# A ring of expert weights with nine places instead of eight, its first places refilled by quarters, and fewer filler products around the last chunk of a mixing

## The reference

```
# first block
merged = sigmoid(mg_h) * (o_h @ w_br_hg) + sigmoid(mg_n) * (o_n @ w_br_nsa)
y = (1 + g1) * (merged @ w_out)
x = layer_norm(ALPHA * x + y) * ln1_g + ln1_b
h = layer_norm(x) * (1 + sc2) + sh2
y = (1 + g2) * hier_moe(h)              # 32 experts, hidden width 512
x = layer_norm(ALPHA * x + y) * ln2_g + ln2_b
# second block
x = x + gt_m * (concat(attn_out, pool_out) @ w_out)
h = modulate(rmsnorm(x, norm_ffn_g), sh_f, sc_f)
x = x + gt_f * hierarchical_moe(h)      # 32 experts, hidden width 256
return rmsnorm(x, norm_final_g)
# both mixtures
group   = argmax of 4 group logits; 2 best of its 8 experts; weight = p_group * softmax(2 logits)
expert  = (silu(h @ w1[e]) * (h @ w3[e])) @ w2[e]
```

## Time and profile before

| what | value |
|---|---|
| median of 3 runs (lowest, highest) | 1993.25 us (1984.94, 2000.85) |
| the profiled execution, and its span | 1992.76 us, 1990.9 us |
| mean granted TensorE clock in it | 0.945 of full speed |
| busy: TensorE products, VectorE, ScalarE, GpSimd | 1742.8, 763.2, 431.6, 103.2 us |
| bytes moved by the DMA engines, mean rate | 474.79 MB, 238 GB/s |
| issued by SP's queue | 398.66 MB |
| one slice of expert weights | 2048 KB, 27.8 to 33.8 us from issue to landing |
| first mixing and its experts, products from, to | 844, 1416 us |
| second mixing and its experts, products from, to | 1629, 1967 us |

### The profile page before, as it was taken

One profiled execution on the slowest core, in us unless ns is written; L12 is line 12 of the kernel. 1 busy time (PEld: TensorE's weight loads), 2 busy tenths in 40 slices (PEclk: granted clock), 3 DMA queues, 4 the chain that ended last, 5 costly groups with the idle time before them and its releaser, 6 DMA issues. The chain is left out here.

```text
span 1990.9 us, 22057 instructions
## 1 busy us (share of the span) xinstructions
PE 1742.8 (88%) x8104; PEld 994.4 (50%) x8104; DVE 763.2 (38%) x1907; ACT 431.6 (22%) x1072; POOL 103.2 (5%) x127
## 2 busy tenths in 40 slices
PE   4999997988998999998977887877889899897886
PEld 2655554445666888747323323333358555632332
DVE  5344445473556654454101111011545454221115
ACT  3323222203445000012201101010122340121122
POOL 1100000000000000000000000000000000011110
PEclk8999997989999999998989989999999999898898
DMA  9533234771111622354999999999611223599995
GB/s 374 192 136 117 96 147 175 266 270 62 40 40 52 231 108 85 144 237 164 383 421 426 427 427 427 427 426 425 246 43 69 86 108 160 205 414 424 424 423 213
DMA packets 68055, 474.79 MB, mean 238 GB/s; under 512 B 11359, under 2 KB 12575, under 8 KB 43249
## 3 DMA queue, kind: packets, MB, share of 16 engines
q1 hardware_dynamic: 51200, 398.66, 49.4%
q0 software_dynamic: 15600, 70.61, 9.3%
q10 hardware_dynamic: 1152, 4.19, 0.5%
HBM read 459.53 MB, written 34.11 MB: 248 GB/s over the span
## 5 line engine op out<-in xcount | busy, mean ns | idle before, releaser
L2105 PE MATMUL moe_ps<-moe_up,moe_hg 128*64 128x512 f32 x1536 | 380.9, 654 | 104.4 <-DMA moe_up<-in_exp_gate 42.8
L2105 PEld LDWEIGHTS moe_ps<-moe_up,moe_hg 128*64 128x64 f32 x1536 | 132.8, 150 | 349.0 <-issue 348.7
L490 PE MATMUL hg_proj<-hT,hg_w 128*128 128x512 f32 x384 | 171.6, 605 | 6.1 <-DMA hg_w<-in_w_hg 6.1
L2142 PE MATMUL moe_ps<-moe_down,moe_midT 128*64 128x512 f32 x720 | 162.7, 601 | 15.6 <-DMA moe_down<-in_exp_down 15.0
L2195 ACT ACTIVATE moe_sig<-moe_ps 128x512 f32<-128x512 f32 (+1 forms) x32 | 15.7, 490 | 545.0 <-PE moe_ps L2105 545.0
L2224 DVE COPY moe_midT<-moe_ps 128x512 f32<-128x512 f32 (+1 forms) x32 | 17.8, 557 | 273.1 <-PE moe_ps L2114 273.1
L490 PEld LDWEIGHTS hg_proj<-hT,hg_w 128*128 128x128 f32 x384 | 73.0, 193 | 94.9 <-issue 87.5
L2234 DVE SCALAR_TENSOR_TENSOR moe_res<-moe_ps,moe_route_slot_share,moe_gain 128x512 f32<-128x512 f32 x64 | 45.1, 746 | 162.3 <-PE moe_ps L2142 162.1
L2142 PEld LDWEIGHTS moe_ps<-moe_down,moe_midT 128*64 128x64 f32 x720 | 54.0, 138 | 103.7 <-issue 102.3
L2180 ACT ACTIVATE moe_hg<-moe_ps,mod,scale_ffn 128x128 f32<-128x128 f32 x248 | 89.9, 467 | 49.1 <-PE moe_ps L2088 49.1
L2216 DVE TENSOR_TENSOR moe_mid<-moe_sig,moe_ps 128x512 f32<-128x512 f32 (+1 forms) x32 | 17.7, 555 | 161.0 <-PE moe_ps L2105 158.2
(11 more groups left out here) (409 smaller groups left out, 2520.8 us busy)
## 6 DMA issues: line engine op xcount, KB each, us to landing
moe_down<-in_exp_down SPq DMA_DIRECT2D x45, 2048.0 KB, 29.0
moe_up<-in_exp_up SPq DMA_DIRECT2D x32, 2048.0 KB, 27.8
moe_up<-in_exp_gate SPq DMA_DIRECT2D x32, 2048.0 KB, 29.2
moe_up<-in_exp_in SPq DMA_DIRECT2D x32, 2048.0 KB, 33.8
rest_w<-in_mod_rest POOLq DMA_DIRECT2D x16, 1536.0 KB, 7.3
hg_w<-in_w_hg SPq DMA_DIRECT2D x32, 512.0 KB, 3.6
rest_w<-in_mod_rest POOLq DMA_DIRECT2D x8, 2048.0 KB, 8.5
xn<-in_w_merge SPq DMA_DIRECT2D x32, 512.0 KB, 4.4
```

The lines of the kernel that those rows point to most:

```text
L490: last = pe.matmul(proj[bank][:, :], w[s][:, kc, :], k.hT[:, kc, :], start=(kc == 0), stop=(kc == KC - 1))
L2105: last = pe.matmul(self.up_ps[u][e * SLOTS:(e + 1) * SLOTS, :], self.hg[m % 2][:, kc, e * SLOTS:(e + 1) * SLOTS], w[:, kc, :], start=(kc = ...
L2142: last = pe.matmul(self.res_ps[side][e * SLOTS:(e + 1) * SLOTS, :], self.midT[:, f, e * SLOTS:(e + 1) * SLOTS], w[e][:, f, side * 512:(sid ...
```

## The change

- The ring has nine places (`N_SLOTS`). The mixing's input and weights keep the last three, so six slices are issued when the stage begins, and three after the eighth half.
- Slices 9 and 10, the first that need a place used before, are loaded by `load_pieces` in four quarters each. A quarter is two of the eight blocks of 128 rows of an `up` slice, or one of four of a `down` slice. SP waits for `first_read`, a new semaphore that TensorE raises behind products kc = 1, 3 and 5 of the first pair, and for `up_done0` ahead of the last quarter. TensorE waits for these two slices on semaphores of their own; the counts of places 0 and 1 are one load lower from there on (`times`). SP goes on in the old way from slice 11.
- In the mixing the counts of fillers change: where `affine` is set from 26, 6 and 24 to 12, 3, 5 and 22, the 5 between the turning of the last chunk and its logits. Where it is None they are 8 and 22, and the last chunk is turned ahead of the third chunk's logits.
- The rows of the norms (`load_rows`) are loaded before SP waits for GpSimd's scatters, in place 6 of the ring (first block) or 5 (second); the results go to places 0 and 1, or 3 and 4.
- Room in SBUF: `SMALL` shrinks from 3584 to 2048 bytes of a partition, and the descriptor space of GpSimd's DMAs is set to 4096 bytes of a partition.

The core of the diff:

```diff
...
@@ -1481,8 +1481,8 @@
 KB = 1024
 SLOT = 16 * KB
-N_SLOTS = 8
-SMALL = 7 * 512
+N_SLOTS = 9
+SMALL = 2048
 NOWHERE = 4096
@@ -1649,12 +1649,18 @@
         logits(1)
         turned(2)
         pe.wait_ge(S["part_free"], 2 * TC - 3)
-        self.keep_warm(pe, 26)
-        logits(2)
-        self.keep_warm(pe, 6)
-        turned(3)
+        if self.affine is not None:
+            self.keep_warm(pe, 12)
+            logits(2)
+            self.keep_warm(pe, 3)
+            turned(3)
+            self.keep_warm(pe, 5)
+        else:
+            self.keep_warm(pe, 8)
+            turned(3)
+            logits(2)
         logits(3)
-        self.keep_warm(pe, 24)
+        self.keep_warm(pe, 22)
     def keep_warm(self, pe, n):
@@ -1939,12 +1945,38 @@
         self.last_slot = len(self.slices) - len(downs(PAIRS - 1))
         self.per_slot = [sum(i % N_SLOTS == s for i in range(self.last_slot)) for s in range(N_SLOTS)]
         self.last_w = memory.slot(f"{tag}_last", self.last_slot % N_SLOTS, [P, 2, self.FC, D])
+        self.pieces_loaded = [k.sem(ctx, f"{tag}_pieces_loaded{n}") for n in range(2)]
         self.last_loaded = [k.sem(ctx, f"{tag}_last_loaded{f}") for f in range(self.FC)]
+
+    def piece(self, i, q):
+
+        what, m, u, e = self.slices[i]
+        s = i % N_SLOTS
+        if what == "up":
+            return self.up_w[s][:, 2 * q:2 * q + 2, :], self.up_v[u][2 * m + e][:, 2 * q:2 * q + 2, :]
+        return self.down_w[s][:, q, :], self.down_v[2 * m + q // 2][:, q % 2, :] if e == 2 else self.down_v[2 * m + e][:, q, :]
+
+    def load_pieces(self, sp):
+
+        for q in range(KC // 2):
+            if q < KC // 2 - 1:
+                sp.wait_ge(self.S["first_read"], q + 1)
+            else:
+                sp.wait_ge(self.S["up_done0"], 1)
+            for n, i in enumerate((N_SLOTS, N_SLOTS + 1)):
+                place, source = self.piece(i, q)
+                sp.dma_start(place, source).then_inc(self.pieces_loaded[n], 16)
+
+    def times(self, i, j):
+
+        s = i % N_SLOTS
+        pieced = 1 if s < 2 and (i >= N_SLOTS or not isinstance(j, int)) else 0
+        return j * 16 * self.per_slot[s] + 16 * (i // N_SLOTS + 1 - pieced)
     def load(self, sp, i, j):
         what, m, u, e = self.slices[i]
         if i >= N_SLOTS or not isinstance(j, int):
-            before, n, part, _ = self.slices[i - N_SLOTS]
+            before, n, part, _ = self.slices[i - N_SLOTS if i >= N_SLOTS else self.final_slice(i)]
             done = self.S["down_done" if before == "down" else f"up_done{part}"]
             sp.wait_ge(done, j * PAIRS + (n + 1 if i >= N_SLOTS else n + 1 - PAIRS))
         s = i % N_SLOTS
@@ -1988,9 +2020,13 @@
                 done()
             sums(False)
+    def final_slice(self, s):
+
+        return max(i for i in range(len(self.slices)) if i % N_SLOTS == s)
+
     def emptied(self, sp, s):
-        what, m, u, _ = self.slices[max(i for i in range(len(self.slices)) if i % N_SLOTS == s)]
+        what, m, u, _ = self.slices[self.final_slice(s)]
         sp.wait_ge(self.S["down_done" if what == "down" else f"up_done{u}"], m + 1)
     def sync(self, sp, begin, added):
@@ -2000,6 +2036,8 @@
                 if isinstance(j, int) and i == 2 * N_SLOTS:
                     added.load_tokens(sp)
             if isinstance(j, int):
+                self.emptied(sp, added.rows_place)
+                added.load_rows(sp)
                 sp.wait_ge(self.S["early_stored"], 1)
                 added.load(sp, self.emptied)
@@ -2074,7 +2113,10 @@
         def ready(j, *slices):
             for s in slices:
                 i = self.at[s]
-                pe.wait_ge(self.loaded[i % N_SLOTS], j * 16 * self.per_slot[i % N_SLOTS] + 16 * (i // N_SLOTS + 1))
+                if isinstance(j, int) and N_SLOTS <= i < N_SLOTS + 2:
+                    pe.wait_ge(self.pieces_loaded[i - N_SLOTS], 16 * (KC // 2))
+                else:
+                    pe.wait_ge(self.loaded[i % N_SLOTS], self.times(i, j))
         def turn_rows(j, m):
             pe.wait_ge(self.x_loaded[m % 2], j * 16 * (PAIRS // 2) + 16 * (m // 2 + 1))
@@ -2104,6 +2146,8 @@
                     w = self.up_w[self.at["up", m, u, e] % N_SLOTS]
                     last = pe.matmul(self.up_ps[u][e * SLOTS:(e + 1) * SLOTS, :], self.hg[m % 2][:, kc, e * SLOTS:(e + 1) * SLOTS],
                                      w[:, kc, :], start=(kc == 0), stop=(kc == KC - 1))
+                if isinstance(j, int) and m == 0 and u == 0 and kc % 2 and kc < KC - 1:
+                    last.then_inc(S["first_read"], 1)
             last.then_inc(S[f"up_done{u}"], 1)
         def turn_mid(j, m):
@@ -2287,9 +2331,11 @@
     def __init__(self, k, ctx, tag, memory, banks, experts, residual, affine, scale=None, shift=None, store=None):
         self.k, self.experts, self.residual, self.affine = k, experts, residual, affine
         self.scale, self.shift, self.store, self.ps = scale, shift, store, banks
-        self.y = [memory.at(f"{tag}_y{c}", memory.ring + 8 * c * KB, [P, 2, D]) for c in range(TC)]
-        self.rows = [memory.at(f"{tag}_row{n}", memory.ring + (32 + 4 * n) * KB, [P, D]) for n in range(2 if store is None else 1)]
-        self.junk = memory.at(f"{tag}_junk", memory.ring + 40 * KB, [P, D])
+        self.y_place, self.rows_place = (0, 6) if store is None else (3, 5)
+        y, rows = (memory.ring + place * SLOT for place in (self.y_place, self.rows_place))
+        self.y = [memory.at(f"{tag}_y{c}", y + 8 * c * KB, [P, 2, D]) for c in range(TC)]
+        self.rows = [memory.at(f"{tag}_row{n}", rows + 4 * n * KB, [P, D]) for n in range(2 if store is None else 1)]
+        self.junk = memory.at(f"{tag}_junk", rows + 8 * KB, [P, D])
         n = experts.kept_pairs
         self.onehot = [memory.at(f"{tag}_onehot{m}", k.hT_at + (16 - 2 * (n - m)) * KB, [P, SEQ]) for m in range(n)]
         if store is None:
@@ -2307,19 +2353,17 @@
     def load_tokens(self, sp):
         sp.dma_start(self.onehot[-1][:], self.k.i["tokens"].partition_broadcast(P)).then_inc(self.tokens_loaded, 16)
+    def load_rows(self, sp):
+        for n, row in enumerate(self.rows):
+            sp.dma_start(row[:], self.k.i["norm_rows"][self.affine + n:self.affine + n + 1, :].broadcast_to([P, D])).then_inc(self.rows_loaded, 16)
+
     def load(self, sp, emptied=None):
-        k = self.k
         view = self.experts.results.rearrange("(s c p) d -> c p s d", s=2, p=P)
         for c in range(TC):
             if emptied is not None and c % 2 == 0:
-                emptied(sp, c // 2)
+                emptied(sp, self.y_place + c // 2)
             sp.dma_start(self.y[c][:], view[c]).then_inc(self.loaded[c], 16)
-            if c == 1:
-                if emptied is not None:
-                    emptied(sp, 2)
-                for n, row in enumerate(self.rows):
-                    sp.dma_start(row[:], k.i["norm_rows"][self.affine + n:self.affine + n + 1, :].broadcast_to([P, D])).then_inc(self.rows_loaded, 16)
     def used(self, sp):
@@ -2573,12 +2617,13 @@
             @block.sync
             def _(sp):
                 out.sync(sp)
-                for i in range(5):
+                for i in range(N_SLOTS - 3):
                     experts.load(sp, i, 0)
                 sp.wait_ge(out.S["done"], 2 * TC)
-                for i in range(5, N_SLOTS):
+                for i in range(N_SLOTS - 3, N_SLOTS):
                     experts.load(sp, i, 0)
-                experts.sync(sp, N_SLOTS, added)
+                experts.load_pieces(sp)
+                experts.sync(sp, N_SLOTS + 2, added)
                 added.sync(sp, send_next)
             @block.gpsimd
@@ -3116,7 +3161,7 @@
     from concourse.bass_utils import run_bass_kernel_spmd
     arrays = {f"in_{n}": a for n, a in arrange(**inputs).items()}
-    nc = bacc.Bacc("TRN2", target_bir_lowering=False, num_devices=1)
+    nc = bacc.Bacc("TRN2", target_bir_lowering=False, num_devices=1, dynamic_dma_scratch_size=4096)
     views = {n[3:]: nc.dram_tensor(n, a.shape, mybir.dt.from_np(a.dtype), kind="ExternalInput").ap() for n, a in arrays.items()}
     out = nc.dram_tensor("out_x", (SEQ, D), F32, kind="ExternalOutput").ap()
     program(nc, views, out)
```

2 lines of the change are left out of this document (1 added, 1 removed).

## The result

The changed kernel takes **1970.18 us** in the median of four runs (1965.93 to 1976.26). The kernel before, with one more run in the same comparison, takes 1996.20. The ratio is 0.9889, interval 0.9851 to 0.9928. The prediction was 1970. By the one 22 us are saved, by the other 18. That is clear of noise, and under 2%. The profiled execution took 1967.43 us.

A forecast was written before the change was run, and what follows sets the result against it. Transfers were taken to bound both expert stages. Savings of 7.4 + 5.0 + 3.5 + 6.2 + 0.7 = 22.8 us from the profiled 1992.8 gave 1970 us, range 1960 to 1985 (8 in 10).

The forecast's parts named there:

- forecast case: Whole kernel: all gains arrive as summed, 1970 us, own range 1963 to 1978; chance 0.65.
- ring, first stage: First expert stage: ninth place and early quarters put it 1.5 slices ahead, saving 7.4 us.
- ring, second stage: Second expert stage: the extra slice alone saves 5.0 us; the quarters' earlier start is lost whole.
- first mixing: Mixing ahead of the first stage: earlier last turning and faster logits and fillers save 3.5 us (1.5 to 4.6).
- second mixing: Mixing ahead of the second stage: last chunk turned before the third's logits, saving 6.2 us (3 to 7).
- sums behind the first stage: Norm rows loaded earlier let VectorE's work behind the first stage move by 0.7 us (0 to 1.9).
- head start: First pair's places refilled after each quarter of its products, so loads start 5.3 us before these end.
- rival of the falling clock: Both mixings: fewer fillers let TensorE's clock fall to 1.2 GHz, some 6.4 us less gain, 1976 us; chance 0.15.
- Quarters dear: Both expert stages: 512 KB transfers pay a fixed part each, costing 10 us in sum, 1980 us; chance 0.07.
- Ninth place nothing: Both expert stages: the extra slice brings nothing, only mixings and sums gain, 10.4 us, 1982 us; chance 0.08.
- descriptor space: GpSimd's smaller space makes its transfers wait for each other, 60 us in the second stage, 2030 us; chance 0.05.

The follow-up runs named there:

- again: The changed kernel profiled and measured once more, nothing altered; 1970.17 us, ratio 0.9908 of the kernel before.
- mixing only: The kernel before with only the mixing's new order and filler counts; 1986.19 us, ratio 0.9965.
- All: The changed kernel with slices 11 and 12 by quarters, fillers in the routing, and 12 fillers between the second stage's first two pairs; 1960.81 us, ratio 0.9864.
- Memory only: The kernel before with only the two new sizes, SMALL 2048 and 4096 bytes of GpSimd descriptor space; 1989.53 us, ratio 1.0006.
- halves: The changed kernel with slices 9 and 10 loaded in two halves each instead of four quarters; 1972.18 us, ratio 0.9914.
- Nine places, whole loads: The changed kernel with slices 9 and 10 loaded whole behind the first pair's products instead of by quarters; 1975.38 us, ratio 0.9917.
- Old mixing: The changed kernel with the mixing's old order and filler counts; 1980.61 us, ratio 0.9933.

## Why the prediction was right

The forecast case came, by its own mechanism, and the total of 22.8 us stands beside 22 and 18 measured. That the median fell on 1970 to 0.2 us is partly luck: the four stretches hold 20.3 and 17.6 us of the 22.1 booked for them, and the kernel before had a median of 1996.2 in this comparison, not 1992.8. The forecast put 0.56 on less than 1973.3 us, which both medians of the changed kernel are; but of the two ratios, 0.9889 and 0.9908, only the first is below 0.99. Its terms, against the traces:

| term | predicted | trace, changed kernel and again |
|---|---|---|
| ring, first stage | 7.4 | 7.5, 7.8 |
| ring, second stage | 5.0 | 5.8, 3.1 |
| first mixing | 3.5 | 1.1, 1.1 |
| second mixing | 6.2 | 5.8, 5.6 |
| sums behind the first stage | 0.7 | 0 |

**The ring, first stage.** Slice and quarters, tried apart, gave 4.9 and 2.7 us, and 7.5 together: they add. The quarters' 2.4 us was worked out as head start less an idle gap behind it, 5.3 - 2.9. The size held, the gap wasn't idle: at 338 GB/s the quarters still flowed when the next loads were issued at 950.44, so what had been put down as a pause was used up by slower transfers. **Second stage.** The slice alone was forecast. The two readings lie on either side of 5.0, and what parts them is the granted clock of the first products. With that clock low in both, nine places take 220.5 and eight 225.9: 5.4 us.

**First mixing.** Here a term was mis-sized: 1.1 us, below its own lower bound of 1.5. The step that failed is where the sum ends, at the choice: it took for granted that what is won there arrives at the first pair's products, and had no term for the counting, the gather and the turning between. TensorE's steps, in us from the turning of the third chunk:

| TensorE begins | before | changed | again | mixing only |
|---|---|---|---|---|
| turning of the last chunk | 9.84 | 7.47 | 7.15 | 7.14 |
| counting, behind the choice | 22.98 | 19.72 | 18.58 | 18.58 |
| placing of the shares | 29.85 | 26.94 | 26.70 | 26.42 |
| turning of the first gathered rows | 32.57 | 31.47 | 31.42 | 30.16 |
| first pair's products | 36.33 | 35.24 | 35.19 | 33.93 |

Rows behind it: one of before, two of the changed kernel again, one of "Mixing only".

```profile
938.05 1.97 PE L2088 MATMUL moe_ps<-consts,moe_xg 128*128 128x128 f32 x8 [0.82 <-DMA moe_xg<-kept_rows,moe_route_slot_rows]
```

```profile
922.39 0.41 PE L1775 MATMUL moe_ps<-moe_route_chosen,consts 128*128 128x32 f32 x2 [1.78 <-DVE moe_route_chosen L1846]
935.23 1.12 PE L2130 MATMUL moe_ps<-consts,moe_xg 128*128 128x128 f32 x4 [2.82 <-DMA moe_xg<-kept_rows,moe_route_slot_rows]
```

```profile
942.64 0.69 PE L2094 MATMUL moe_ps<-consts,moe_xg 128*128 128x128 f32 x2 [1.85 <-DMA moe_xg<-kept_rows,moe_route_slot_rows]
```

With the clock at 1.00 up to the counting (again, and "Mixing only") the forecast's own steps gave 4.4 us there, near its upper bound of 4.6. Then TensorE took 8.1 us from counting to shares, where before it took 6.9, as the clock fell earlier in that stretch (counting, 1.56 us for 1.06). And it waited 2.82 us for the first gathered rows where it had waited 0.82. From issue to the turning these rows took 3.6 us before and 5.4 and 5.6 in the two traces of the changed kernel. They took 3.5 to 3.6 in all three traces with the old mixing, 4.6 to 5.6 in all seven with the new one and no fillers in the routing, and 3.5 in the three with fillers. It isn't a full queue: the DMA engines of the changed kernel moved nothing from 917.0 to 926.5, and the gather was issued at 925.28.

```profile
917.00:926.50 9.50, 3.87 (x54) 3.45 (x52) 5.36 (x22) 0.21 (x1) 1.11 (x1) 0.79 0.00 0
```

Nor is it how early the issue comes: in "All" it came 25.6 us behind the third chunk's turning, as in "Mixing only", and the rows took 3.5 us for 4.6. What makes them late stays open.

In the first trace of the changed kernel something else happened besides: the granted clock fell to 0.50, 1.2 GHz, from some 905.4 to 908.9 (0.72 in the window 905 to 906, 0.50 in the next two, 0.57 up to 909), after the logits' wait of 0.59 us. The last chunk's turning began 0.4 us after its xn (906.27), where the forecast allowed 0.1, and turning and fillers took nearly twice as long. That cost 1.1 us at the counting, but 0.05 us at the first pair's products, since the wait for the gathered rows took it up.

**Second mixing.** 5.8 for 6.2, 5.6 to 6.2 in the other traces with the new mixing and no fillers in the routing. That the logits' 4.08 us cover ScalarE's work holds. The rival of the falling clock did not come in this mixing, where the clock held through turning and logits. In the first mixing it came in four of the ten traces with the new order (turnings of 1.9 to 2.0 us), the first of the changed kernel among them. That 1.1 us stayed there, near the 1.5 which this rival had named, is no support for it: the second trace, without the fall, has the same 1.1. Turning alone doesn't bring the fall, as the Trainium skill's rule on transposes (TensorE: Matmul & The Clock Gate, Part 4) might have it: in "Mixing only" the last chunk's turning ran at 1.00, and so did the fillers and logits before and behind it.

**The sums.** The 0.7 us did not come. VectorE no longer waits for the third piece of results, but TensorE took its place. VectorE in the changed kernel, against the earlier trace rows, and TensorE ahead of it:

```profile
1407.35 1.22 DVE L2392 TENSOR_TENSOR moe_add_y<-moe_add_y 128x1024 f32<-128x1024 f32 x1
...
1410.69 1.29 DVE L1545 BATCH_NORM_STATS2 moe_add_n_stats<-moe_ps 128x6 f32<-128x512 f32 x2 [2.11 <-PE moe_ps L2443]
```

```profile
1403.47 5.40 PE L2443 MATMUL moe_ps<-moe_add_y,consts 128*128 128x512 f32 x8 [2.42 <-DVE moe_add_y L2397]
```

From the last up products to these statistics it takes 26.04 us, where before it took 1425.62 - 1399.57 = 26.05. The prediction had TensorE ready at about 1424.9 and let only VectorE move; but TensorE's own work moved too. These eight took 0.68 us each, where the eight behind them, from 1408.70, took 0.45. Over all traces this stretch takes 25.1 to 26.3 us with the new order of loads, and 26.1, 25.3 and 23.9 in the three with the old one (before, "Mixing only", "Memory only"). So nothing was gained here, and 1 us may have been lost; the loads' order was not tried alone.

**Quarters dear.** Their transfers are slower, 338 GB/s against 390 of halves, so the rival's mechanism exists; it costs nothing since the time lost is time in which the queue would have been idle. What the prediction held against it, the 423 GB/s of the earlier trace rows, was misread: the four 512 KB loads were issued in that window, but they landed some 25 us after their issue, and what flowed was for the most part earlier loads of 1 MB. The loads (KB each, median us from issue to landing), and the window in which they flowed:

```profile
hg_w<-in_w_hg SPq DMA_DIRECT2D x4, 512.0 KB, 25.4
```

```profile
34.20:39.49 5.29, 4.02 (x5) 1.83 (x6) 4.34 (x11) 1.55 (x2) 0.58 (x2) 0.50 0.99 400
```

So queued 512 KB loads moved 400 GB/s, and the eight quarters, issued into an empty queue, 338.

**Ninth place nothing** and **descriptor space** fall by "Nine places, whole loads" and "Memory only".

What stays open: why the first gathered rows land later behind the new first mixing, why the granted clock falls in some executions and not in others of one kernel, and what makes up the 836 to 850 us ahead of the first mixing.

## What to carry to other kernels

Where a stage is bound by its transfers, count the slices that are in when its saturated stretch starts: one more ring place is worth one slice's transfer at the stage's own rate, 2,097 KB at 424 GB/s, if the queue is idle while it loads. Refilling the first freed place early was worth its head start less the gap up to the next free place, so look for that gap, and open the next place early too. Follow a gain on to the instruction that the stage waits for: of 4.4 us won at the choice, 1.1 arrived at the first products. Judge such parts by stretches between fixed instructions of the trace, not by whole spans: the same kernel's start moved by 5 us here, a quarter of what the change is worth.

## What the runs showed of the hardware

- TensorE's granted clock fell to 0.50 behind a wait of 0.59 us between narrow products in the first mixing of the changed kernel, and stayed at 1.00 in the same place, behind the same wait, in the second trace of that kernel and in "Mixing only". So whether it falls isn't set by the instructions alone.
- Behind a wait of 3.2 us in the second stage the second pair's products took 8.4 to 9.9 us instead of 7.09 in nine of thirteen traces (granted clock 0.72 over 12.4 us in "Old mixing"); 12 fillers in the wait, with the fillers in the routing, kept 1.00 in the one trace of "All". The low clock at the start of that stage cost some 2.7 us.
- Loads of 512 KB issued in pairs into an empty queue moved 338 GB/s, of 1 MB 390, of 2 MB 381 (over 7 to 12 us, the first slow ones included), and 512 KB loads that stood in the queue 400.
- The same indirect gather, issued with the DMA engines idle, reached TensorE after 3.5 us in some kernels and after 4.6 to 5.6 us in others that differ in what TensorE did ahead of it.
